# The compression branch of a sparse attention: its blocks are built by GpSimd, and its two inner layers stand in two column tiles of TensorE

## The reference, cut to what matters

```python
cmp_idx = arange(n_cmp)[:, None] * 16 + arange(32)[None, :]     # n_cmp = 15 blocks of 32 tokens, 16 apart
def compress(t, pe, w1, w2):                                    # t: (B, G=2, T=256, 64)
    blk = (t[:, :, cmp_idx] + pe).reshape(B, G, n_cmp, 32 * 64) # pe: (32, 64), the position terms
    return silu(blk @ w1) @ w2                                  # w1: (2048, 64), w2: (64, 64)
k_cmp = compress(kc, pe_k, phi_k1, phi_k2)
v_cmp = compress(vc, pe_v, phi_v1, phi_v2)
s_cmp = einsum('bghtd,bgcd->bghtc', q, k_cmp) * scale           # then a masked softmax, then @ v_cmp
```

## Time and profile before

| | us |
|---|---|
| median of 3 runs | 1714.91 (1714.83 to 1716.19) |
| the profiled execution, its own time | 1716.06 |
| its span in the trace | 1714.3 |
| mean granted TensorE clock | 0.983 |
| the attention part with the compression, layer 0 of the second family | about 883 to 954 |
| the same, layer 1 | about 1420 to 1492 |

### The profile page before, as it was taken

The page is one execution under the profiler, slowest core; times in us unless marked ns, Lnnn a source line. Parts: engine busy times, 40 slices in busy tenths (PEclk is TensorE's granted clock), DMA queues, the critical chain, the costliest instruction groups (busy, mean ns, idle before and its releaser), DMA issues.

```text
span 1714.3 us, 25092 instructions
## 1 busy us (share of the span) xinstructions
PE 1638.3 (96%) x9954; PEld 1402.0 (82%) x9954; DVE 1092.7 (64%) x1391; ACT 877.5 (51%) x1309; POOL 59.9 (3%) x110
## 2 busy tenths in 40 slices
PE   7999999989999999999998999999999998899997
PEld 7878888977888878888876888888888896688886
DVE  5766656686765666656666565657665666666554
ACT  5555444655544455444546454445444555554443
POOL 1000000010000020000000000002000000000000
PEclk9999999999999989999989999999999998999999
DMA  8324555642555557555530255557555541045551
GB/s 280 123 75 171 172 196 173 200 131 66 170 191 193 177 175 232 171 196 174 170 99 2 99 173 195 186 186 220 196 186 185 187 131 48 15 151 197 185 196 67
DMA packets 211151, 271.74 MB, mean 159 GB/s; under 512 B 4824, under 2 KB 191824, under 8 KB 211072
## 3 DMA queue, kind: packets, MB, share of 16 engines
q1 hardware_dynamic: 208208, 263.39, 46.1%
q0 software_dynamic: 2544, 7.09, 1.8%
q10 hardware_dynamic: 320, 0.18, 0.0%
HBM read 269.58 MB, written 1.05 MB: 158 GB/s over the span
## 4 chain that ended last, share of the span: by engine, by line
PE 87%; DVE 7%; ACT 3%; issue 2%; DMA 1%; POOL 0%; DVEq 0%; SPq 0%; POOLq 0%; ACTq 0%
PE pair L1754 29%; PE pair L1756 15%; PE bank L1682 12%; PE bank L1684 12%; PE bank L1683 12%; PE bank L1883 1%; PE pair L1864 1%; DVE probs L1164 1%; ACT probs L782 1%; PE bank L1913 1%; ACT w_hi L656 1%; DMA raw<-in_w_mem_kv 1%; DVE negmax L1128 1%; PE bank L1830 1%; DVE w_lo L999 1%
## 5 line engine op out<-in xcount | busy, mean ns | idle before, releaser
L1754 PE MATMUL pair<-xt,w_hi 128*128 128x512 f32 x2112 | 753.2, 400 | 3.8 <-DVE xt L1008 3.8
L999 DVE TENSOR_TENSOR w_lo<-raw,w_hi 128x2048 fp32r<-128x2048 f32 x248 | 567.9, 2290 | 155.9 <-ACT w_hi L656 154.5
L656 ACT ACTIVATE w_hi<-raw 128x2048 fp32r<-128x2048 f32 x248 | 474.2, 1914 | 281.7 <-PE pair L1756 200.9
L1756 PE MATMUL pair<-xt,w_lo 128*128 128x256 f32 x2112 | 594.3, 281 | 0.0
L1754 PEld LDWEIGHTS pair<-xt,w_hi 128*128 128x128 f32 x2112 | 398.8, 189 | 103.6 <-issue 5.2
L1756 PEld LDWEIGHTS pair<-xt,w_lo 128*128 128x128 f32 x2112 | 400.8, 190 | 2.3
L1682 PE MATMUL bank<-w_hi,hid_hi 128*128 128x512 f32 x528 | 207.3, 393 | 0.0
L1682 PE MATMUL bank<-w_hi,xt 128*128 128x256 f32 x720 | 206.2, 286 | 0.4 <-DVE xt L1008 0.4
L1684 PE MATMUL bank<-w_lo,hid_hi 128*128 128x512 f32 x528 | 206.4, 391 | 0.0
L1683 PE MATMUL bank<-w_hi,hid_lo 128*128 128x512 f32 x528 | 205.8, 390 | 0.0
L1684 PE MATMUL bank<-w_lo,xt 128*128 128x256 f32 x720 | 203.7, 283 | 0.0
(11 more groups left out here) (271 smaller groups left out, 1422.7 us busy)
## 6 DMA issues: line engine op xcount, KB each, us to landing
raw<-in_w_gate_up SPq DMA_DIRECT2D x44, 1024.0 KB, 5.1
raw<-in_ffn_wg SPq DMA_DIRECT2D x44, 1024.0 KB, 5.1
raw<-in_ffn_wu SPq DMA_DIRECT2D x44, 1024.0 KB, 5.1
raw<-in_ffn_wd SPq DMA_DIRECT2D x44, 1024.0 KB, 5.0
raw<-in_w_in SPq DMA_DIRECT2D x30, 1024.0 KB, 5.3
raw<-in_w_down SPq DMA_DIRECT2D x22, 1024.0 KB, 5.0
raw<-in_w_o SPq DMA_DIRECT2D x8, 1024.0 KB, 5.4
raw<-in_w_out SPq DMA_DIRECT2D x8, 1024.0 KB, 5.3
```

Source lines behind the costliest of these rows:

```text
L656: act.activation(w_hi[s][:, :], raw[s][:, :], ACT.Copy).then_inc(hi_ready, 1)
L999: dve.tensor_tensor(w_lo[s][:, :], raw[s][:, :], w_hi[s][:, :].bitcast(F32), ALU.subtract)\
L1754: pe.matmul(out[:, 512 * m:512 * (m + 1)], w[0][:, c, cols], xt[:, 2 * SEQ * c:2 * SEQ * (c + 1)], start=(c == 0), stop=False)
L1756: last = pe.matmul(out[:, 512 * m + SEQ:512 * (m + 1)], w[1][:, c, cols], hi_half(xt, c), start=False, stop=(c == KC - 1))
```

## The change

DVE's `blocks` is taken from the steps 1 and 2 and put into POOL's program, as the same sixteen instructions per layer, on a semaphore of its own (`blocks_ready`). POOL waits for the windows `kc 1` and `vc 1`, and before the first block also for `pe_t` and for the rotation of `kw`, whose scratch is the place of `blk`. PE now waits for both sets of blocks before its first product. It then takes the products of keys and values in turn: those of the keys write the PSUM partitions 0 to 63, those of the values 64 to 127. So the hidden values lie on 128 partitions x 30 columns and not on 64 x 60, and the five small instructions between the layers work on that shape. The second layer's weights for the values lie on the partitions 64 to 127.

```diff
-        hid_c, hid_e = (sb(n, 60, at=m_base + 1376 + 256 * i) ...)
+        hid_c, hid_e = (sb(n, 30, at=m_base + 1376 + 256 * i) ...)
 # POOL
+            def blocks(l, w):
+                pool.wait_ge(heads_out_v.sem, heads_out_v.at((l, True, ("kc 1", "vc 1")[w])))
+                if w == 0:
+                    pool.wait_ge(task_out_v.sem, task_out_v.at((l, "pe")))
+                    pool.wait_ge(prep_ready.sem, prep_ready.at(("heads", l, "kw")))
+                b4 = blk[w][:, :].rearrange("p (o g n) -> p g n o", o=16, g=B_G)
+                for q in range(2):
+                    ...
+                    for c in range(2):
+                        ...
+                        for g in range(B_G):
+                            pool.tensor_tensor(
+                                b4[rows_, g, :, 8 * c:8 * c + 8], seg[:, g, :, :, q],
+                                term.unsqueeze(1).to_broadcast([HD, N_CMP, 8]), ALU.add)\
+                                .then_inc(blocks_ready.sem, blocks_ready.mark((l, w)))
...
-                        (phi2[0:HD, HD * w:HD * (w + 1)], a[f"nsa_phi_{which}2_2"][l]),
+                        (phi2[HD * w:HD * (w + 1), 0:HD], a[f"nsa_phi_{which}2_2"][l]),
...
                 power([(12, 14, A_QR), (14, 16, A_KVR)], ("latent", l))
+                for w in range(2):
+                    blocks(l, w)
 # DVE (the same function is taken away there), and ACT's exponential on hid_e[:, :]
-                         (1, "end"): [lambda: blocks(0)], (2, "end"): [lambda: blocks(1)],
-                    link(dve.tensor_scalar(hid_e[0:HD, :], QT_B[0:HD, 0:60], -1.0, 87.0, ALU.mult, ALU.min),
+                    link(dve.tensor_scalar(hid_e[:, :], QT_B[:, 0:30], -1.0, 87.0, ALU.mult, ALU.min),
 # PE, cmp1
                         for w in range(2):
-                            pe.wait_ge(prep_ready.sem, prep_ready.at(("blk", l, w)))
-                            for o in range(16):
-                                last = pe.matmul(out[0:HD, 30 * w:30 * w + 30], phi1[w][:, HD * o:HD * (o + 1)],
+                            pe.wait_ge(blocks_ready.sem, blocks_ready.at((l, w)))
+                        for o in range(16):
+                            for w in range(2):
+                                last = pe.matmul(out[HD * w:HD * (w + 1), 0:30], phi1[w][:, HD * o:HD * (o + 1)],
                                                  blk[w][:, 30 * o:30 * (o + 1)], start=(o == 0), stop=(o == 15))
 # PE, cmp2
-                                             hid_c[0:HD, 30 + N_CMP * g:30 + N_CMP * (g + 1)],
-                                             phi2[0:HD, HD:2 * HD], start=True, stop=True)
+                                             hid_c[HD:P, N_CMP * g:N_CMP * (g + 1)],
+                                             phi2[HD:P, 0:HD], start=True, stop=True)
```

More of the change, by code:

```diff
@@ L306, in build @@
         pe_t = sb("pe_t", 2 * 16, at=m_base + 1248)
-        hid_c, hid_e = (sb(n, 60, at=m_base + 1376 + 256 * i) for i, n in enumerate(("hid_c", "hid_e")))
+        hid_c, hid_e = (sb(n, 30, at=m_base + 1376 + 256 * i) for i, n in enumerate(("hid_c", "hid_e")))
         lat_t = sb("lat_t", 6 * P, at=f_base + 23 * 1024)
@@ L424, in build @@
             sig(n) for n in ("heads_turned", "heads_out_a", "heads_out_v"))
+        blocks_ready = sig("blocks_ready")
         heads_out = {"scalar": heads_out_a, "vector": heads_out_v}
@@ L584, in _ @@
                 .then_inc(tables_landed, 16)
+            def blocks(l, w):
[5 more added lines that the diff above has]
+                for q in range(2):
+                    rows_ = slice(HD * q, HD * (q + 1))
+                    kc = kcv_t[:, SEQ * (2 * w + 1 - q):SEQ * (2 * w + 3 - q)].rearrange("p (g s) -> p g s", g=B_G)
+                    for c in range(2):
+                        seg = kc[rows_, :, 16 * c:16 * c + 240].rearrange("p g (n o l) -> p g n o l", o=8, l=2)
+                        term = pe_t[rows_, 16 * w + 8 * c:16 * w + 8 * c + 8]
+                        for g in range(B_G):
[3 more added lines that the diff above has]
+                                .then_inc(blocks_ready.sem, blocks_ready.mark((l, w)))
             def norm(j, source=squares):
@@ L946, in hidden_exp @@
                     act.wait_ge(prep_ready.sem, prep_ready.at(("cmp", l)))
-                    act.activation(hid_e[0:HD, :], hid_e[0:HD, :], ACT.Exp)\
+                    act.activation(hid_e[:, :], hid_e[:, :], ACT.Exp)\
                        .then_inc(small_act.sem, small_act.mark(("cmp", l)))
@@ L1519, in places_out @@
                     link(dve.tensor_copy(pe_t[:, :], QT_B[:, 0:32]), task_out_v, (l, "pe"))
[L1521 to L1534, removed]
-                                   .then_inc(prep_ready.sem, prep_ready.mark(("blk", l, w)))
                 def hidden_guarded():
                     dve.wait_ge(small_mm.sem, small_mm.at(("cmp1", l)))
-                    link(dve.tensor_scalar(hid_e[0:HD, :], QT_B[0:HD, 0:60], -1.0, 87.0, ALU.mult, ALU.min),
+                    link(dve.tensor_scalar(hid_e[:, :], QT_B[:, 0:30], -1.0, 87.0, ALU.mult, ALU.min),
                          prep_ready, ("cmp", l))
@@ L1545, in hidden_sigmoid @@
                     dve.wait_ge(small_act.sem, small_act.at(("cmp", l)))
-                    link(dve.tensor_scalar(hid_e[0:HD, :], hid_e[0:HD, :], 1.0, None, ALU.add))
-                    link(dve.reciprocal(hid_e[0:HD, :], hid_e[0:HD, :]))
-                    link(dve.tensor_tensor(hid_c[0:HD, :], QT_B[0:HD, 0:60], hid_e[0:HD, :], ALU.mult),
+                    link(dve.tensor_scalar(hid_e[:, :], hid_e[:, :], 1.0, None, ALU.add))
+                    link(dve.reciprocal(hid_e[:, :], hid_e[:, :]))
+                    link(dve.tensor_tensor(hid_c[:, :], QT_B[:, 0:30], hid_e[:, :], ALU.mult),
                          task_out_v, (l, "cmp1"))
```

## The result

The changed kernel takes 1707.38 us (median of 5 runs, 1705.38 to 1707.91) against 1714.91 us (median of 5, 1714.83 to 1716.57): a ratio of 0.9949, 95% interval 0.9935 to 0.9964, 7.5 us less. A second series gave 1707.76 against 1716.34, 0.995 (0.9936 to 0.9963). I had predicted 1707.6. The profiled execution took 1707.91 us, the longest of its five, with a span of 1706.1, 8.2 less than before; the one before was 1.15 us above its median.

The account below looks back on a forecast made before the run. TensorE, busy 96% of the span, was taken as the bound. Waits 1.6, `cmp1` 3.6, small instructions 0.6 and clock 1.5 sum to 7.3 us, giving 1707.6 us against 1714.91; range 1704 to 1712.

Parts of the forecast that it names:

- The waits: TensorE's waits of 0.82 and 0.80 us ahead of pair 1's turning vanish when blocks leave VectorE: 1.6 us.
- GpSimd's price: Sixteen block additions per layer on GpSimd at 0.5 us each, 8 us in all, hidden ahead of `cmp1`: zero cost.
- the deadline: Start of `cmp1`, by which GpSimd's sixteen instructions must end: 13.5 us, 0.85 us each; missing it had 12%.
- The fill: GpSimd's fill of 128 columns, 0.22 us, taken as nearest row; an addition should cost two or three fills.
- the power: GpSimd's power, 160 ns per column, the upper bound for an addition: 20 us for one instruction.
- `cmp1`: Alternating column tiles load weights side by side: 2.1 us instead of 3.87, 3.6 us in all; failing had 10%.
- Four rows of `cmp2`: Four weight loads at the start of `cmp2` took 0.20 us, read as column tiles loading side by side.
- The small instructions: Between the two inner layers, 30 columns instead of 60 shorten the chain and the wait ahead of `kw`: 0.6 us.
- the spare: Slack of 1.3 us between pair 1's division on VectorE and TensorE's coming for it, covering delays by GpSimd blocks.
- The clock: Half clock around pair 1's turning ends sooner in one of two layers: 1.5 us; lengthening instead had 5%.
- 0.81 for faster: Probability that the whole kernel comes out faster than the limit of 1711.5 us, summed over forecast and rivals.

Follow-up runs that it names:

- Experiment 2: Changed kernel with the sixteen block instructions back on VectorE, column tiles kept: 1713.23 us, 0.998 of the kernel before.
- Experiment 4: Changed kernel with GpSimd computing all blocks a second time and `cmp1` waiting for that pass: 1716.32 us, 0.9999 of the kernel before.
- experiment 8: Changed kernel with gates and rotation moved to step 3, where GpSimd also waits for pair 1's division before its first block: 1700.00 us, 0.991 of the kernel before.
- experiment 3: Changed kernel with all products of the keys first, then those of the values, each in its own column tile: 1712.55 us, 0.9979 of the kernel before.
- experiment 5: Changed kernel with VectorE's gates and rotation of `kw` moved from step 0 to the end of step 3: 1700.85 us, 0.991 of the kernel before.
- the filled kernel before: Kernel before with three never-read products put ahead of pair 0's turning in the second family: 1714.42 us, 0.999 of the kernel before.
- experiment 1: Kernel before with only the blocks moved to GpSimd, `cmp1` as it was: 1712.85 us, 0.9977 of the kernel before.
- experiment 7: Changed kernel with the second eight block instructions (the values') of each layer back on VectorE: 1706.56 us, 0.9944 of the kernel before.
- the filled changed kernel: Changed kernel with three never-read products put ahead of pair 0's turning in the second family: 1706.47 us, 0.9944 of the kernel before.
- experiment 9: Kernel before, blocks on VectorE and one column tile, with gates and rotation moved to the end of step 3: 1711.12 us, 0.9972 of the kernel before.

## Why the prediction was right, and where a size was off

**The waits (1.6 predicted).** Right. 0.82 and 0.80 us are gone, and for the reason given: TensorE comes from its own window. Experiment 2 brings them back with the instructions.

**GpSimd's price (0.5 us per instruction, hidden).** Right at 0.51, and the deadline as well. Experiment 4 went past it, and the waits came at `cmp1`. The fill was the right neighbour and the power the wrong one. The 13.5 us were sized at the old clock, though: in layer 1, where the clock returns earlier, the spare is 2.9 us and not 5, and in experiment 8 it is 0.5. Whatever speeds up the work between the start and the deadline takes from the cover.

**`cmp1` (3.6 predicted, 2.1 us each).** Right: 3.7, 2.01 each. Four rows of `cmp2` were enough to tell that two column tiles load side by side, and experiment 3 shows that the order is what pays.

The Trainium skill ("TensorE: Matmul & The Clock Gate", section "Back-to-back issue gap") gives an issue floor of about 25 ns for a matmul of up to 64 columns, and about 62 ns where hardware decode is off. Here 64 matmul instructions took 2.01 us, 31 ns each: more than the first figure and half of the second, which did not bind.

**The small instructions (0.6 predicted).** 0.5: the reciprocal takes 0.34 us, which my slope put at 0.35, and `kw` waits 0.63.

**VectorE beside GpSimd.** I had argued the loss for GpSimd only and left VectorE to the spare. VectorE lost 0.25 us on the division and 0.2 on the small product ahead of it (0.44, 0.23 before). The spare covered both, so it cost nothing here; but it was nearer than the text says, since 1.3 us had become 0.7. In experiment 5 the cover is gone, and the same contention costs 0.5 us per layer, which experiment 8 gets back. The Trainium skill ("SBUF — State Buffer", section "Who interferes with whom") names the exclusion of a VectorE instruction with two inputs in SBUF and a GpSimd instruction that reads SBUF. These runs agree for the division and give its size.

**The clock (1.5 predicted, ends +3.4 and -1.7).** Here the size was off. I gave the gain to one of the two layers. Over all profiles, A is 25.1 us on average with the first blocks on VectorE (before, experiment 2 and the filled kernel before; six values, 24.31 to 25.91), and 22.6 with them on GpSimd (changed twice, experiments 1, 3 and 7 and the filled changed kernel; twelve values, 21.15 to 23.66). That is 2.5 us per layer, 0.8 of it the wait and 1.7 the clock: 3.4 for both, the upper end of what I allowed. My price was also read too high: by the row that it names (0.87 for 1.54 us) 3.5 us at half clock become 2.0 and not 1.8, a gain of 1.5 per layer and not 1.7. The 1.7 us per layer come about because the low stretches are 3.9 us shorter on average, 8.0 against 11.9. In the two profiles first compared the clock's share is 5.0 - 1.6 = 3.4 as well, nearly all of it in layer 1, and that split is partly luck: before, layer 1 has the late fall (see below) and the changed kernel the early one. Profiles with the late fall on both sides have 25.4 and 23.2 us. So the predicted 1707.6 stands beside 1707.38 partly because this gain, some 2 us too small, stood against losses elsewhere that the sum didn't have: 7.3 predicted, 9.2 in the two attention parts, 7.5 in the medians. The second series, with 8.6, is 1.3 us more than I predicted.

**What the prediction overlooked.** TensorE also waits ahead of pair 0's turning, 0.99 us in layer 0 (until 891.28) and 2.31 us in layer 1:

```profile
1428.39 0.84 PE L1883 MATMUL bank<-cst,probs 128*128 128x128 f32 x6 [2.31 <-DVE probs L1164]
```

The windows of the earlier trace rows begin behind these waits, and the prediction says nothing of them, though the second is TensorE's longest there. Experiment 5 shows that shortening them is worth nearly as much as the whole change. Two smaller slips of the prediction: the parts that are said to make 0.81 for faster add up to 0.83, and the upper end of the range, by its own terms, is 1712.7 and not 1712.

**What stays open.** Which rule brings the clock down and back. The 13 profiles have 26 attention parts, and the rows show where the clock falls in them. In 11 it falls early, 3.6 to 5.5 us behind the first mask product and ahead of pair 0's turning; the one pause up to there is a wait of 1.22 us that every kernel has. In 10 it falls late, 9.9 to 10.3 us behind, just after pair 0's turning, ahead of which TensorE waited 2.31 us (1.73 with the filling). In one, layer 0 of experiment 9, it falls behind the 2.31 us ahead of pair 1. The same kernel has either kind, from layer to layer and from profile to profile, so the difference is not the kernel's. In four parts, both layers of experiments 5 and 8, where no pause ahead of a turning is above 0.7 us, it doesn't fall. That speaks for the long pause as the cause of the late fall. For the early one it shows nothing: it comes before the wait of pair 0, layer 1 of experiment 9 has it with the same move, and that four profiled parts were free of it may be luck. My sentence that the rise comes behind work without a pause is not a rule either: 6.8 us of such work passed at 0.50. That filling pauses would help isn't shown.

## What to carry to other kernels

When many small matmuls are bound by their weight loads, put pairs of them into two column tiles and let neighbours in the program alternate; tiles alone do little (3.66 us of 3.87, against 2.01 in turn). Before an engine's task is moved to GpSimd, look at which of it the other engine really waits for, and keep it from running beside a VectorE product of two operands that somebody waits for. Where a stretch runs at half clock, look at the longest wait ahead of it, and at more than one profile, since the place where the clock falls changes from one to the next: the move that shortened TensorE's pause of 2.31 us to 0.32 was worth 6.9 us, nearly as much as the whole change studied here.

## What the runs showed of the hardware

- Two column tiles of 64 columns load weights side by side: 64 instructions in 2.01 us, 31 ns each, against 60 ns in one tile (3.87 us). With the products in turn starts lie within 10 ns; with one tile after the other, 3.66 us.
- GpSimd adds two strided inputs of 64 x 120 in 0.51 us on average beside a busy VectorE (16 instructions in 8.19 us; the middle one of 32 takes 0.454, the longest 0.902), and in 7.37 / 16 = 0.46 us when it starts behind the division of pair 1.
- VectorE's product of two operands (the two instructions of a division) takes 1.03 us without GpSimd's additions beside it and 1.28 to 1.47 with them; its small product of 128 x 4 with one operand per partition takes 0.44 us there and 0.23 in the kernel before.
- The granted clock was 0.50 for 6.8 us in which TensorE was busy throughout. A stretch of 18.7 us of which TensorE was idle for 2.9 had 1.00 throughout. In layer 0 of the changed kernel the clock fell 3.6 us into the attention part in one profile and 10.2 us into it in the other.
